# Splitting fp32 weight units into a high and a low part: one 128x1024 instruction per engine instead of two of 128x512, in a two-block transformer kernel

## The reference, cut to what matters

```python
proj = h @ w_in[l]                              # 1024 x 5640 and 1024 x 5896
y = sigmoid(ga) * (y_a @ w_branch_a[l]) + ...   # 512 x 1024 each
x = x + gt1 * (y @ w_out[l])
q = xb @ w_pq                                   # 1024 x 2048
# PEER: 16384 experts, 16 of them for each token and head
s_top, i_top = lax.top_k(s, PEER_TOPK)
...
act = jax.nn.gelu(jnp.einsum("thkd,td->thk", u_exp[e], xb))
out = jnp.einsum("thk,thkd->td", gate * act, v_exp[e])
```

## Time and profile before

| | |
|---|---|
| median of 3 runs | 2700.23 us |
| span of the profiled execution (the page gives no other time of it) | 2693.1 us |
| PE matmul busy | 2399.2 us, 89% |
| PE weight load busy | 2298.4 us, 85% |
| VectorE busy | 1850.1 us, 69% |
| ScalarE busy | 1327.6 us, 49% |
| GpSimd busy | 196.7 us, 7% |
| mean granted TensorE clock | 0.924 |
| raw units: time from issue to landing | 3.3 to 3.5 us |
| DMA | 145 GB/s mean |

### The profile page before, as it was taken

One profiled execution on the slowest core, in us unless ns is written; L12 is line 12 of the kernel. 1 busy time (PEld: TensorE's weight loads), 2 busy tenths in 40 slices (PEclk: granted clock), 3 DMA queues, 4 the chain that ended last, 5 costly groups with the idle time before them and its releaser, 6 DMA issues.

```text
span 2693.1 us, 54111 instructions
## 1 busy us (share of the span) xinstructions
PE 2399.2 (89%) x18096; PEld 2298.4 (85%) x18096; DVE 1850.1 (69%) x3632; ACT 1327.6 (49%) x2906; POOL 196.7 (7%) x158
## 2 busy tenths in 40 slices
PE   3887699999986799999889888899999966899998
PEld 2885589999986699999879847899999965899998
DVE  7675655888869965555643456548888699755555
ACT  2344244455546655545544563345554466545544
POOL 3000000000005500000010000000000054100000
PEclk7998799999997699999989989899999967899999
DMA  8761144555540045555434403445555500355554
GB/s 313 267 221 54 47 149 146 181 181 184 181 148 0 0 156 180 183 183 180 142 108 161 144 0 110 133 141 187 180 179 187 180 0 0 106 183 180 183 182 148
DMA packets 106071, 389.61 MB, mean 145 GB/s; under 512 B 12032, under 2 KB 12160, under 8 KB 105232
## 3 DMA queue, kind: packets, MB, share of 16 engines
q1 hardware_dynamic: 104688, 381.73, 43.0%
q10 hardware_dynamic: 992, 4.88, 0.5%
q0 software_dynamic: 320, 2.13, 0.2%
HBM read 387.64 MB, written 1.05 MB: 144 GB/s over the span
## 4 chain that ended last, share of the span: by engine, by line
PE 78%; DVE 14%; issue 3%; ACT 3%; DMA 1%; DVEq 1%; SPq 0%; ACTq 0%
PE ps L541 18%; PE ps L510 15%; PE ps L505 15%; PE ps L507 15%; PE ps L545 9%; DVE big L1339 4%; DVE scores L1331 3%; DVE scores L1327 1%; DVE big L1126 1%; PE ps L620 1%; PE ps L600 1%; DMA big<-ada_in 1%; DVE act_lo L1179 1%; DVE lo L1103 1%; PE ps L648 1%
## 5 line engine op out<-in xcount | busy, mean ns | idle before, releaser
L835 ACT ACTIVATE hi<-raw 128x512 fp32r<-128x512 f32 x1356 | 776.0, 620 | 91.4 <-PE ps L510 86.9
L1103 DVE TENSOR_TENSOR lo<-raw,hi 128x512 fp32r<-128x512 f32 x844 | 553.2, 697 | 190.1 <-ACT hi L835 189.1
L505 PE MATMUL ps<-act_hi,hi 128*128 128x256 f32 x3376 | 556.7, 288 | 82.1 <-DVE act_lo L1179 41.9
L510 PE MATMUL ps<-act_hi,lo 128*128 128x256 f32 x3376 | 554.1, 287 | 27.5 <-DVE lo L1103 27.5
L505 PEld LDWEIGHTS ps<-act_hi,hi 128*128 128x128 f32 x3376 | 477.3, 197 | 88.7 <-DVE act_lo L1179 67.0
L507 PE MATMUL ps<-act_lo,hi 128*128 128x256 f32 x3376 | 551.9, 286 | 0.0
L541 PE MATMUL ps<-act_hi,hi 128*128 128x256 f32 x2048 | 513.9, 283 | 0.0
L541 PE MATMUL ps<-act_lo,hi 128*128 128x256 f32 x2048 | 513.5, 283 | 0.0
L510 PEld LDWEIGHTS ps<-act_hi,lo 128*128 128x128 f32 x3376 | 475.5, 196 | 30.4 <-DVE lo L1103 30.2
L507 PEld LDWEIGHTS ps<-act_lo,hi 128*128 128x128 f32 x3376 | 475.8, 196 | 0.0
L860 ACT ACTIVATE big<-ps 128x256 f32 (+1 forms) x354 | 135.7, 383 | 588.6 <-PE ps L510 588.6
(11 more groups left out here) (178 smaller groups left out, 1506.0 us busy)
## 6 DMA issues: line engine op xcount, KB each, us to landing
raw<-u SPq DMA_DIRECT2D x256, 512.0 KB, 3.3
raw<-v SPq DMA_DIRECT2D x256, 512.0 KB, 3.5
raw<-front SPq DMA_DIRECT2D x166, 512.0 KB, 3.3
big<-ada_in SPq DMA_DIRECT2D x48, 512.0 KB, 5.5
big<-biasA_in ACTq DMA_DIRECT2D x1, 2048.0 KB, 10.7
xT<-xT_in ACTq DMA_DIRECT2D x1, 1024.0 KB, 9.6
big<-keys_in ACTq DMA_DIRECT2D x1, 1024.0 KB, 14.0
scores<-memT_in POOLq DMA_DIRECT2D x1, 1024.0 KB, 6.8
```

Source lines behind the costliest of these rows:

```text
L505: pe.matmul(out_ap, hi_l(k), hi_r(k), start=(first and k == 0), stop=False, skip_group_check=True)
L510: mm = pe.matmul(out_ap, lo_l(k), hi_r(k), start=False, stop=(last and k == n - 1), skip_group_check=True)
L835: act.activation(hi[:, s, :, :], raw[:, rs, 4 * h:4 * h + 4, :], ACT.Copy).then_inc(hi_done, 1)
L1103: dve.tensor_tensor(lo[:, s, :, :], raw[:, rs, 4 * h:4 * h + 4, :], hi[:, s, :, :].bitcast(F32), ALU.subtract).then_inc(lo_done, 1)
```

## The change

The rings hold two whole units (`RING` = 2) of the same bytes in all. ScalarE makes hi of a unit in one 128x1024 instruction, VectorE lo in one. `hi_done` and `lo_done` count units; `used` still counts halves, and ScalarE waits until both halves of the unit two before are used. TensorE waits for hi and for lo only in a unit's first half. In the K runs VectorE evicts two halves behind each unit's lo. `weight_lo_static` goes; `experts` calls `weight_lo`.

```diff
-RING = 4
+RING = 2
...
-        hi = sb("hi", [P, RING, 4, P], F32R)
-        lo = sb("lo", [P, RING, 4, P], F32R)
+        hi = sb("hi", [P, RING, KT, P], F32R)
+        lo = sb("lo", [P, RING, KT, P], F32R)
...
-                sp.wait_ge(lo_done, (n - RAW + 1) * 2)
+                sp.wait_ge(lo_done, n - RAW + 1)
...
             def half(r, g, j, h):
-                m = (g * GROUP + j) * 2 + (r.half0 + h)
-                s = (r.half0 + 2 * j + h) % RING
-                pe.wait_ge(hi_done, m + 1)
+                m = g * GROUP + (r.unit0 + j)
+                s = (r.unit0 + j) % RING
+                if h == 0:
+                    pe.wait_ge(hi_done, m + 1)
 
                 def wait_lo():
-                    pe.wait_ge(lo_done, m + 1)
+                    if h == 0:
+                        pe.wait_ge(lo_done, m + 1)
...
-            def weight_hi(r, g, j, h):
-
-                m = (g * GROUP + j) * 2 + (r.half0 + h)
-                s = (r.half0 + 2 * j + h) % RING
+            def weight_hi(r, g, j):
+
+                m = g * GROUP + (r.unit0 + j)
+                s = (r.unit0 + j) % RING
                 rs = (r.unit0 + j) % RAW
-                if h == 0:
-
-                    act.wait_ge(raw_in[rs], g * 16 + 16 * ((r.unit0 + j) // RAW + 1))
+                act.wait_ge(raw_in[rs], g * 16 + 16 * ((r.unit0 + j) // RAW + 1))
                 if not (is_static(m) and m < RING):
-                    act.wait_ge(used, m - RING + 1)
-                act.activation(hi[:, s, :, :], raw[:, rs, 4 * h:4 * h + 4, :], ACT.Copy).then_inc(hi_done, 1)
+                    act.wait_ge(used, m * 2 - 2 * (RING - 1))
+                act.activation(hi[:, s, :, :], raw[:, rs, :, :], ACT.Copy).then_inc(hi_done, 1)
...
-            def weight_lo(r, g, j, h):
-
-                m = (g * GROUP + j) * 2 + (r.half0 + h)
-                s = (r.half0 + 2 * j + h) % RING
+            def weight_lo(r, g, j):
+
+                m = g * GROUP + (r.unit0 + j)
+                s = (r.unit0 + j) % RING
                 rs = (r.unit0 + j) % RAW
                 dve.wait_ge(hi_done, m + 1)
-                dve.tensor_tensor(lo[:, s, :, :], raw[:, rs, 4 * h:4 * h + 4, :], hi[:, s, :, :].bitcast(F32),
+                dve.tensor_tensor(lo[:, s, :, :], raw[:, rs, :, :], hi[:, s, :, :].bitcast(F32),
                                   ALU.subtract).then_inc(lo_done, 1)
...
-                        for h in range(2):
-                            weight_lo(r, g, j, h)
-                            if evict and per == 2 and not (is_static(g) and g == 0 and j == 0 and h == 0):
-                                out(g * GROUP * 2 + (2 * j + h - 1), (r.out0 + 2 * j + h - 1) % 2)
+                        weight_lo(r, g, j)
+                        if evict and per == 2 and not (is_static(g) and g == 0 and j == 0):
+                            for h in range(2):
+                                out(g * GROUP * 2 + (2 * j + h - 2), (r.out0 + h) % 2)
...
                 if evict:
+                    if per == 2:
+                        out(r.outs - 2, (r.out0 + r.outs - 2) % 2)
                     out(r.outs - 1, (r.out0 + r.outs - 1) % 2)
...
                 for u in range(r.units):
-                    for h in range(2):
-                        weight_lo_static(r, u, h)
+                    weight_lo(r, u // GROUP, u % GROUP)
```

More of the change, by code:

```diff
@@ L524, in half @@
                     c0 = 4 if r.name in ("branch_b", "swa_o") else 0
-                    mm = three(po[o], lambda k: hi[:, s, k, :], lambda k: lo[:, s, k, :],
+                    mm = three(po[o], lambda k: hi[:, s, k0 + k, :], lambda k: lo[:, s, k0 + k, :],
                                lambda k: act_hi[:, c0 + k, :], lambda k: act_lo[:, c0 + k, :], 4, True, True, wait_lo)
@@ L540, in half @@
                         for w, a in ((hi, act_hi), (hi, act_lo)):
-                            pe.matmul(acc[:, k0 + k, :], w[:, s, k, :], a[:, b, :], start=False, stop=False,
+                            pe.matmul(acc[:, k0 + k, :], w[:, s, k0 + k, :], a[:, b, :], start=False, stop=False,
                                       skip_group_check=True)
@@ L544, in half @@
                     for k in range(4):
-                        mm = pe.matmul(acc[:, k0 + k, :], lo[:, s, k, :], act_hi[:, b, :], start=False, stop=False,
+                        mm = pe.matmul(acc[:, k0 + k, :], lo[:, s, k0 + k, :], act_hi[:, b, :], start=False, stop=False,
                                        skip_group_check=True)
@@ L842, in body @@
                     for j in range(min(GROUP, r.units)):
-                        for h in range(2):
-                            weight_hi(r, g, j, h)
+                        weight_hi(r, g, j)
                         if evict and not (j == 0 and is_static(g) and g == 0):
```

## The result

The changed kernel takes **2737.52 us** (median of 4 runs, 2735.07 to 2742.64), the kernel before in the same comparison 2697.69. The ratio is 1.0147, 95% interval 1.0131 to 1.0162: slower by 1.5%, 40 us. The forecast was 2739. The profiled execution took 2739.37 us, 1.8 more than its span, which is 44.5 us longer than the one in the earlier trace rows. All ratios leave out one execution, of the first experiment's kernel, that took 4731 us for no reason that a trace shows.

The account below looks back on a forecast made before the run. TensorE was taken to set the time in the 512 expert units. Terms of 21.8, 7.3, 3.8, 1.5, 3.2 and 1.0 us sum to 38.6, giving span 2731.7 and time 2739 us; range 2717 to 2758.

Parts of the forecast that it names:

- The wide instructions: ScalarE's copy and VectorE's subtraction at 128x1024: 1056 and 1225 ns, freeing 57 and 44 us in all, off the path.
- u1 and u2, 21.8 us: Expert runs: whole lo queued behind pairs and experts steps is 0.63 and 0.05 us late, 0.68 per 7 units.
- The upper bound of this term: In u1 and u2, with the pairs' durations (1.14, 1.29), the two latenesses come to about 1.17, 37 us.
- Starts behind an evicting ScalarE, 0.75 each: Six run starts where ScalarE evicts before copying: hi 0.44 and lo 0.31 later, 4.5 us of the 7.3 for starts.
- the start behind modulation work (run qkb): One run start that stands behind modulation work on VectorE too: 1.0 us, within the 7.3 for starts.
- Modulation: VectorE's modulation steps inside runs: TensorE waits 0.91 us more at three places, 0.535 at two early ones; 3.8 us.
- convolution: A convolution step of 3.25 us inside a run makes a lo 0.73 us late, twice: 1.5 us.
- starts behind VectorE: Six run starts behind VectorE's own split of the activations: lo 0.535 us later each, 3.2 us, bounds 2 and 4.
- K runs: VectorE evicts two halves behind each whole lo: about 0.05 us for each of 20 units, 1 us, bounds 0 and 4.
- the two early places: Two early modulation places inside runs: TensorE waits 0.535 us longer at each, within the 3.8 us.
- The rival that stalls lower the clock: In the front, longer waits cause three to ten more slow starts, 5 to 17 us more, 2750; chance 0.13.
- main case: The main forecast: lateness of hi and lo makes TensorE wait, 38.6 us in sum, 2739 us; chance 0.76.

Follow-up runs that it names:

- the first experiment: The changed kernel with lo made and counted by halves again (two 128x512 subtractions), hi still one wide copy: 2711.89 us, 1.0053 against the kernel before.

## Why the prediction was right

**The wide instructions.** Estimated at 1.056 and 1.225 us from like rows, measured 1.049 and 1.234. Both errors are under 1%. The saved busy time, ScalarE's above all, was rightly put off the path.

**u1 and u2, 21.8 us.** Measured 0.71 x 32 = 22.7 by the periods, and 21.6 by the experiment that takes the long steps away. TensorE's busy share in u1 is shown as 98%; by the count of matmuls (2700 for 2794) it is the 97% of the forecast. The upper bound of this term was worked out wrongly: with 1.14 and 1.29 in the same steps, lo behind pairs is ready at 614.95, 0.91 late, and lo behind experts in time, which makes 29 us and not 37. The top of the stated range, 2758, was that much too high. Run u1 as a whole, from its first matmul to the transposes behind it, grew by only 10.05 us: its start spends less time at half clock, 1.2 us over the first eight groups. The Trainium skill (Perfetto Trace Analysis, Optimizing Scalar/DVE Operations) has both sentences that were weighed against each other; the runs bear out the one that breaking up instructions may let work be completed sooner, since neither engine was saturated (69% and 49% busy before) and the 66.6 us saved bought nothing.

**Starts behind an evicting ScalarE, 0.75 each.** Timeline of the changed kernel at the start of mv, which answers to the earlier trace rows:

```profile
1384.22 2.00 ACT L835 ACTIVATE hi<-raw 128x1024 fp32r<-128x1024 f32 x2
1385.30 2.36 DVE L1101 TENSOR_TENSOR lo<-raw,hi 128x1024 fp32r<-128x1024 f32 x2 [4.53 <-ACT hi L835]
...
1385.41 0.71 PE L505 MATMUL ps<-act_hi,hi 128*128 128x256 f32 x4 [1.51 <-ACT hi L835]
...
1386.58 0.53 PEld L510 LDWEIGHTS ps<-act_hi,lo 128*128 128x128 f32 x4 [0.19 <-DVE lo L1101]
```

The wait for hi is 1.51 for 1.08, +0.43 as forecast (0.44). lo then holds the first weight load too, and that is worth 0.24 where 0.31 were forecast: from one start to the next, sk to sv, 4.18 us became 4.85, so a start costs 0.67 and not 0.75, 0.5 us less over six starts. At the start behind modulation work (run qkb) only hi's 0.43 is seen, where 1.0 was forecast.

**Modulation, convolution, starts behind VectorE, K runs.** Timeline of the changed kernel at one place of each (the earlier trace rows answer):

```profile
120.84 0.74 PE L510 MATMUL ps<-act_hi,lo 128*128 128x256 f32 x4 [2.09 <-DVE lo L1101]
...
197.73 0.74 PE L510 MATMUL ps<-act_hi,lo 128*128 128x256 f32 x4 [0.50 <-DVE lo L1101]
...
326.59 1.22 PE L505 MATMUL ps<-act_hi,hi 128*128 128x256 f32 x4 [7.48 <-DVE act_lo L1179]
...
345.04 1.23 PE L505 MATMUL ps<-act_hi,hi 128*128 128x256 f32 x4 [4.83 <-DVE act_lo L1179]
...
348.04 1.22 PE L510 MATMUL ps<-act_hi,lo 128*128 128x256 f32 x4 [0.92 <-DVE lo L1101]
```

The wait of 1.20 in qkb is 2.09 (+0.89, forecast 0.91), and so at two more places; at the two early places, forecast at 0.535 each, the waits show no growth (5.40 and 7.53 us in the changed kernel, 5.82 and 8.39 before). The convolution step makes a new wait and 12.26 us from 197.73 to 209.99 where there were 11.52 (+0.74, forecast 0.73). The start behind VectorE's split waits 0.92 where the same one waited 0.39 (+0.53, forecast 0.535); four starts show it, six were forecast. The run of four K units from 326.59 takes 18.45 us for 18.23 (+0.22, forecast 4 x 0.05). Added up by place that is some 13.5 us (starts behind ScalarE 6.2, modulation 2.7, convolution 1.5, starts behind the split 2.1, K runs 1.1) where 16.8 were forecast. The ratio of the kernel with short steps says 18 for the same, so some 4 us are not in these waits (the interval of that ratio is as wide).

**The clock.** The rival that stalls lower the clock was given 0.13. It is wrong for u1, whose clock stays 1.00 through waits of 0.3 to 0.5 us every 21. (The Trainium skill, TensorE: Matmul & The Clock Gate, What's actually happening, says that activity releases the throttle; these rows agree.) It is right in part in the fronts (all that is ahead of u1, and the stretch from mk to u2). Timeline of TensorE at the start of the run fv, the kernel before and then the changed one:

```profile
1440.62 0.71 PE L505 MATMUL ps<-act_hi,hi 128*128 128x256 f32 x4 [1.08 <-ACT hi L835]
1441.16 0.64 PE L507 MATMUL ps<-act_lo,hi 128*128 128x256 f32 x4
...
1442.60 0.64 PE L507 MATMUL ps<-act_lo,hi 128*128 128x256 f32 x4
```

```profile
1468.70 0.71 PE L505 MATMUL ps<-act_hi,hi 128*128 128x256 f32 x4 [1.51 <-ACT hi L835]
...
1471.27 1.05 PE L507 MATMUL ps<-act_lo,hi 128*128 128x256 f32 x4
1472.12 1.05 PE L510 MATMUL ps<-act_hi,lo 128*128 128x256 f32 x4
1472.98 1.05 PE L505 MATMUL ps<-act_hi,hi 128*128 128x256 f32 x4
```

Groups of four at 1.05 us and 0.85 apart, for 0.64 and 0.48: TensorE is at the lower level for four groups, 1.5 us. The kernel with short steps and the wide split shows the same there; the two that split one part by halves, and the kernel before, do not. The start of gates1 has three or four such groups too, in the changed kernel and in each kernel that widens one part, and none in the kernel before. These two starts are some 3 us of clock that came with the longer waits, which the forecast had put at nothing in its main case.

They are not the only ones. In a projection one matmul starts 0.12 us behind the last at full clock and 0.21 behind it at the lower level. Counted over both fronts, the profile of the kernel before has 228 of the second kind, the two others by halves (whole release, short steps) 262 and 270, and the one with only hi wide 263. The three in which lo is wide have 343 (short steps), 350 (lo alone) and 358 (the change). At 0.09 us each that is 7 to 12 us more where lo is wide, the size that this rival had named. The attention and the rest of the work between the projections takes 294 us in two of these three profiles and 300 in the third, for 297 to 300 in those by halves, so a part may be given back there. It is one profile of each kernel, and no experiment held the clock fixed: that wide lo brings more slow starts is what the counts suggest, and how much of the 40 us it makes is open.

**Where the sum was lucky.** The terms outside u1 and u2 were put some 3 us too high, and the clock at nothing; the two errors lean against each other, so the sum is closer than its parts. The 1.5 us between 2739 and 2737.52 also hold a starting point 2.5 us too high (2700.23, and 2697.69 beside the changed kernel). By landmarks the 44.5 us of the spans are 19.5 up to the start of u1 (at 442.80, before 423.29), 10.05 in u1, 7.2 from the first matmul of mk to u2, 10.07 in u2, and -2.3 in the rest. The forecast's terms that lie ahead of u1, its own start included, come to about 10. The kernel with short steps, whose front is the changed one's word for word, reaches u1 at 436.83, and the two kernels by halves (whole release, and short steps on the kernel before) reach it at 428.40 and 428.49: 8.4 us apart, a little under the share forecast. Against these, the profile of before was 5 us short at this point and that of after 6 us long. The medians, 40 us apart, bear the sum of 38.6; the two spans alone would have said 44.5.

## What to carry to other kernels

Merging two instructions into one saves their fixed cost and takes away the early half of the result. Before merging, find the consumer's deadline in the timeline: if it waits for the first half, or if a long step is queued between the producer's instructions, the saving is on an idle engine and the loss is on the busy one. The same view shows the cheap gain: a producer's first work for the next run belongs ahead of its last housekeeping for this one, if the buffers allow it.

## What was not expected of the hardware

The profile's busy time of the matmuls understates short stalls: in u1 5.85 us idle stand for 94 matmuls, 11.3 us; in the kernel with only the wide hi 0.25 us stand for 36, 4.3 us. And the granted clock at a run's start is not fixed by the program alone: with the same instructions ahead of it, the first four matmuls behind the first attention took 1.22 us in the profile of the changed kernel and 0.74 in the one with short steps, and profiles with the same front stand 5 to 6 us apart at its end.
